# Attention outputs kept as token rows: records in DRAM, merged by token tile, memory keys and values on chip

## What is computed

```python
q = rmsnorm(q.reshape(B, S, N_ATT_HEADS, ATT_HEAD_DIM), q_g)
k = rmsnorm(k.reshape(B, S, N_ATT_HEADS, ATT_HEAD_DIM), k_g)
for g, (window, dilation) in enumerate(DIL_GROUPS):
    o, lse = dilated_window_attention(q[:, :, hs], k[:, :, hs], v[:, :, hs], dilation, radius, slopes[hs])
w = jax.nn.softmax(jnp.stack(lses, axis=0), axis=0)
o = jnp.sum(w[..., None] * jnp.stack(outs, axis=0).astype(jnp.float32), axis=0)
```

## Time and profile before

| | us |
|---|---|
| median of 3 runs (2603.51 to 2604.8) | 2604.01 |
| the profiled execution | 2601.91 |
| its span from first to last instruction | 2600.3 |
| PE busy in the span | 2414.0 |
| DVE busy | 1200.4 |
| ACT busy | 981.0 |
| POOL busy | 444.2 |

### The profile page before, as it was taken

How to read it: one execution, slowest core, us unless ns; L and a number is a source line. 1 busy time by engine, 2 the same in 40 slices (tenths; PEclk the granted TensorE clock), 3 DMA queues, 4 the chain that set the end, 5 groups by cost and what they waited for, 6 DMA issues and landing times. The chain is left out here.

```text
span 2600.3 us, 37949 instructions
## 1 busy us (share of the span) xinstructions
PE 2414.0 (93%) x14495; PEld 2088.1 (80%) x14495; DVE 1200.4 (46%) x1766; ACT 981.0 (38%) x1644; POOL 444.2 (17%) x306
## 2 busy tenths in 40 slices
PE   5999998999899999999989889399999999999997
PEld 4876675666688888888878778289999999999997
DVE  6334346445433230000154443756666666666663
ACT  6333334334510002211120033255565656565553
POOL 0001110110200000000000000123444343434342
PEclk8999998999999999999989999689999999999998
DMA  5310000001011112222155354477888878888872
GB/s 170 101 29 25 17 25 17 17 17 49 1 41 41 35 29 82 91 74 91 67 162 167 127 187 154 155 237 240 253 250 263 252 240 252 250 256 261 253 235 60
DMA packets 328237, 342.67 MB, mean 132 GB/s; under 512 B 11857, under 2 KB 308817, under 8 KB 327633
## 3 DMA queue, kind: packets, MB, share of 16 engines
q1 hardware_dynamic: 315280, 309.96, 37.9%
q0 software_dynamic: 12864, 31.46, 4.6%
HBM read 297.35 MB, written 44.04 MB: 131 GB/s over the span
## 5 line engine op out<-in xcount | busy, mean ns | idle before, releaser
L2042 PE MATMUL bank_pair<-tokens_hi_lo,ehi 128*128 128x320 f32 x2048 | 533.1, 347 | 1.1 <-DVE tokens_hi_lo L1886 1.1
L2043 PE MATMUL bank_pair<-tokens_hi_lo,elo 128*128 128x160 f32 x2048 | 483.5, 236 | 0.0
L2043 PEld LDWEIGHTS bank_pair<-tokens_hi_lo,elo 128*128 128x128 f32 x2048 | 391.9, 191 | 0.0
L2042 PEld LDWEIGHTS bank_pair<-tokens_hi_lo,ehi 128*128 128x128 f32 x2048 | 385.2, 188 | 1.2 <-issue 1.2
L1821 ACT ACTIVATE ehi<-eraw 128x2048 fp32r<-128x2048 f32 x192 | 366.1, 1907 | 12.9 <-DMA eraw<-in_w_eg 10.0
L1879 DVE TENSOR_TENSOR elo<-eraw,ehi 128x2048 fp32r<-128x2048 f32 x144 | 329.1, 2286 | 82.8 <-ACT ehi L1821 82.8
L1797 POOL TENSOR_TENSOR elo<-eraw,ehi 128x2048 fp32r<-128x2048 f32 x47 | 225.0, 4788 | 387.0 <-ACT ehi L1821 387.0
L2042 PE MATMUL bank_pair<-hidden_hi_lo,ehi 128*128 128x320 f32 x1024 | 271.8, 349 | 19.1 <-DVE hidden_hi_lo L1892 19.1
L2043 PE MATMUL bank_pair<-hidden_hi_lo,elo 128*128 128x160 f32 x1024 | 241.4, 236 | 0.0
L2042 PEld LDWEIGHTS bank_pair<-hidden_hi_lo,ehi 128*128 128x128 f32 x1024 | 191.9, 187 | 23.3 <-DVE hidden_hi_lo L1892 22.1
L1206 PE MATMUL bank_pair<-hT_hi,whi 128*128 128x512 f32 (+1 forms) x576 | 204.0, 354 | 1.2 <-PEq L1036 1.2
(11 more groups left out here) (254 smaller groups left out, 4326.7 us busy)
## 6 DMA issues: line engine op xcount, KB each, us to landing
eraw<-in_w_eg SPq DMA_DIRECT2D x64, 1024.0 KB, 7.2
eraw<-in_w_eu SPq DMA_DIRECT2D x64, 1024.0 KB, 5.4
eraw<-in_w_ed SPq DMA_DIRECT2D x64, 1024.0 KB, 5.3
raw<-in_w_in SPq DMA_DIRECT2D x64, 512.0 KB, 4.1
scratch_g<-sig SPq DMA_DIRECT2D x24, 640.0 KB, 3.5
sig<-scratch_g SPq DMA_DIRECT2D x24, 640.0 KB, 3.9
xt<-in_x SPq DMA_DIRECT2D x10, 512.0 KB, 4.5
scratch_m<-acc SPq DMA_DIRECT2D x8, 640.0 KB, 4.9
```

Source lines behind the costliest of these rows:

```text
L2042: nc.tensor.matmul(out, wh, moving[:, k, :], start=(k == 0), stop=False)
L2043: ins = nc.tensor.matmul(out[:, HI], wl, moving[:, k, HI], start=False, stop=(k == KD - 1))
```

## The change

The weights of the combination no longer come from logarithms in rows. V of an attention unit now has the (unnormalised) probabilities as weights and the values as moving operand, so its output has the queries on partitions. ACT copies it into a record `orec` of 132 elements for each query: the 128 outputs of two heads, their negative maxima and their sums. POOL writes each record to DRAM (`save_record`); six records take turns, and `biased_max` of a unit waits until the record six units before is saved. The logarithm, the inverse, the subtraction, the multiplication on POOL and piece L are gone for attention units; they stay, but for L and the subtraction, in memory units.

The groups are merged for each segment of tokens in four stages of a tick each: POOL loads the three groups' records of the segment's tokens (`load_rows`), DVE and ACT take minimum, differences and exponentials (`combine_shifts`), DVE the weights (`combine_weights`), POOL multiplies and adds (`merge_rows`), PE transposes the merged rows (`rows_transposes`) and DVE copies them into `oB` (`rows_copy`). The three segments of a pair share the buffer `orows`. For pair 0 the stages lie in ticks 48 to 57, for pair 1 in ticks 72 to 81. Memory keys and values are written once to `Kx` and `Vx` and stay there. The memory units start at tick 68: 15 of the 20 are under products, five come after them, in ticks 75 and 76. The diff, cut to its core:

```diff
-    OT = at("OT", [P, 3, NT], F32, W)
-    LS = at("LS", [2, 3, NT], F32, W + 15360)
...
+    REC = P + 4
+    OUTS, NMAX, SUMS = slice(0, P), slice(P, P + 2), slice(P + 2, P + 4)
+    NREC = 6
...
+    orows = place("head_rows", [P, 4, 3, REC])
+    Kx = place("Kx", [P, XH, NMEM])
+    Vx = place("Vx", [P, 4, XH * P])
...
+    orec = [place(f"head_record{i}", [P, REC]) for i in range(NREC)]
...
+    scratch_o = nc.dram_tensor("scratch_o", [2, NT, 3, REC], F32, kind="Internal").ap()
...
         if ph % 3 == 2:
-            for i in range(4):
-                ticks[start + room + 1 + i]["combine"].append((ph // 3, i))
-            after = start + room + 5
-    for i in range(n_units - 60):
-        ticks[after + i // 5]["units"].append(60 + i)
+            for n in range(3):
+                for stage in range(4):
+                    ticks[start + room + 4 + 3 * n + stage]["combine"].append((ph // 3, n, stage))
+    for j in range(XH):
+        first_tick = start + 4 + 2 * j + (j == 3)
+        for i in range(5):
+            ticks[first_tick + i // 3]["units"].append(60 + 5 * j + i)
...
-            if u is not None and u < 60:
-                acts.append(("lse", u))
...
-                if c == 11:
-
-                    sp.wait_ge(seg_free, 8)
-                    sp.wait_ge(s_vcp, 4)
-                    sp.dma_start(scratch_kx, Kx_early[:].rearrange("p a b -> p (a b)")).then_inc(s_memout, 16)
-                    sp.dma_start(scratch_vx, Vx_early[:].rearrange("p a b -> p (a b)")).then_inc(s_memout, 16)
-            sp.wait_ge(s_memout, 32)
-            sp.wait_ge(pv_done, N_ATT)
-            sp.dma_start(Kx[:].rearrange("p a b -> p (a b)"), scratch_kx).then_inc(s_memin, 16)
-            sp.dma_start(Vx[:].rearrange("p a b -> p (a b)"), scratch_vx).then_inc(s_memin, 16)
...
-                    nc.scalar.activation(dst, obank[:, 0:P], ACT.Copy).then_inc(o_copied, 1)
+                    nc.scalar.activation(orec[v % NREC][:, OUTS], obank[:, 0:P], ACT.Copy).then_inc(o_copied, 1)
...
+            def save_record(v):
                 un = unit(v)
+                pool.wait_ge(o_copied, v + 1)
+                pool.dma_start(scratch_o[un["pair"], tok(None, un["base"], un["st"]), un["g"], :],
+                               orec[v % NREC][:]).then_inc(rec_saved[v % NREC], 16)
...
+            def load_rows(pr, n):
+                t0, nt = SEGS[n]
+                c = 3 * pr + n
+                if n == 0:
+                    for i in range(NREC):
+                        pool.wait_ge(rec_saved[i], 16 * (30 // NREC) * (pr + 1))
+                if c >= 1:
+                    pool.wait_ge(rows_tr, c)
+                pool.dma_start(orows[:, 0:nt // P],
+                               scratch_o[pr, t0:t0 + nt].rearrange("(n p) g r -> p n g r", p=P)).then_inc(
+                    rows_loaded, 16)
+
+            def merge_rows(pr, n):
+                c, nn = 3 * pr + n, SEGS[n][1] // P
+                rec = orows[:, 0:nn]
+                pool.wait_ge(c_wts, c + 1)
+                for i in range(nn):
+                    heads = rec[:, i, :, OUTS].rearrange("p g (h e) -> p g h e", h=2)
+                    ins = nc.gpsimd.tensor_tensor(heads, heads,
+                                                  c_wt[:, i].unsqueeze(3).to_broadcast([P, 3, 2, E_ATT]), ALU.mult)
+                step(ins)
+                step(nc.gpsimd.tensor_tensor(rec[:, :, 0, OUTS], rec[:, :, 0, OUTS], rec[:, :, 1, OUTS], ALU.add))
+                nc.gpsimd.tensor_tensor(rec[:, :, 0, OUTS], rec[:, :, 0, OUTS], rec[:, :, 2, OUTS],
+                                        ALU.add).then_inc(rows_merged, 1)
+
+            for tk in ticks:
+                for what, v in tk["amid"] + tk["after"]:
+                    if what == "values" and v < N_ATT:
+                        save_record(v)
+                    elif what == "scores" and v >= N_ATT:
+                        normalise(v)
+                for pr, n, stage in tk["combine"]:
+                    if stage == 0:
+                        load_rows(pr, n)
+                    elif stage == 2:
+                        merge_rows(pr, n)
...
-                    dve.wait_ge(p_norm, v - 2)
+                neg = nmax[:, b:b + 2]
                 if un["att"]:
+                    neg = orec[v % NREC][:, NMAX]
+                    if v >= NREC:
+                        dve.wait_ge(rec_saved[v % NREC], 16 * (v // NREC))
...
+            def combine_shifts(pr, n):
+                c, nn = 3 * pr + n, SEGS[n][1] // P
+                rec, lowest = orows[:, 0:nn], c_min[:, 0:nn]
+                dve.wait_ge(rows_loaded, 16 * (c + 1))
+                step(nc.vector.tensor_tensor(lowest, rec[:, :, 0, NMAX], rec[:, :, 1, NMAX], ALU.min))
+                step(nc.vector.tensor_tensor(lowest, lowest, rec[:, :, 2, NMAX], ALU.min))
+                nc.vector.tensor_tensor(c_wt[:, 0:nn], lowest.unsqueeze(2).to_broadcast([P, nn, 3, 2]),
+                                        rec[:, :, :, NMAX], ALU.subtract).then_inc(c_dsub, 1)
...
+            def rows_copy(pr, n):
+                t0, nt = SEGS[n]
+                dve.wait_ge(rows_tr, 3 * pr + n + 1)
+                nc.vector.tensor_copy(oB[:, pr, t0:t0 + nt], tbank[:, 0:nt]).then_inc(rows_cp, 1)
...
-                pe.wait_ge(p_norm, v + 1)
+                if un["att"]:
+                    pe.wait_ge(ex_done, v + 1)
+                else:
+                    pe.wait_ge(p_norm, v - N_ATT + 1)
...
-                            ins = nc.tensor.matmul(obank[64 * h:64 * h + 64, 0:P],
-                                                   V[un["buf"]][0:ln, i, 64 * h:64 * h + 64],
-                                                   PT[v % 2][0:ln, 2 * h + c, :], start=(c == 0),
+                            ins = nc.tensor.matmul(obank[:, 64 * h:64 * h + 64], PT[v % 2][0:ln, 2 * h + c, :],
+                                                   V[un["buf"]][0:ln, i, 64 * h:64 * h + 64], start=(c == 0),
                                                    stop=(c == len(un["keys"]) - 1))
...
+            def rows_transposes(pr, n):
+                pe.wait_ge(rows_merged, 3 * pr + n + 1)
+                free_tbank(("c", 3 * pr + n))
+                for i in range(SEGS[n][1] // P):
+                    ins = nc.tensor.transpose(tbank[:, i * P:(i + 1) * P], orows[:, i, 0, OUTS], ident[:])
+                ins.then_inc(rows_tr, 1)
```

More of the change, by code:

```diff
@@ new lines, in kernel_body, with place @@
+    OUTS, NMAX, SUMS = slice(0, P), slice(P, P + 2), slice(P + 2, P + 4)
+    NREC = 6
+    o = W + 37888
+    def place(name, shape):
+        nonlocal o
+        t = at(name, shape, F32, o)
+        size = 4
+        for n in shape[1:]:
+            size *= n
+        o += -(-size // 32) * 32
+        return t
+    orows = place("head_rows", [P, 4, 3, REC])
+    Kx = place("Kx", [P, XH, NMEM])
+    Vx = place("Vx", [P, 4, XH * P])
+    vT = place("vT", [P, NT])
+    sq = [place(f"sq{i}", [P, 512]) for i in range(2)]
@@ L206, in kernel_body @@
+    Pm = [place(f"Pm{i}", [P, 2, 256]) for i in range(3)]
+    PT = [place(f"PT{i}", [P, 4, P]) for i in range(2)]
+    orec = [place(f"head_record{i}", [P, REC]) for i in range(NREC)]
+    c_min = place("combine_min", [P, 4, 2])
+    c_wt = place("combine_weight", [P, 4, 3, 2])
+    c_part = place("combine_part", [P, 4, 3, 2])
+    c_tot = place("combine_total", [P, 4, 2])
     memT_hi = at("memT_hi", [P, KD, NMEM], F32R, W)
     memT_lo = at("memT_lo", [P, KD, NMEM], F32R, W + 16384)
-    Kx_early = at("Kx_early", [P, XH, NMEM], F32, W + 32768 + 2048 + 1024)
@@ L524, in kernel_body @@
         uses += [("u", v) for what, v in tk["after"] if what == "transposes"]
+        uses += [("c", 3 * pr + n) for pr, n, stage in tk["combine"] if stage == 3]
         for use in uses:
@@ L655, in _, with step @@
         @block.gpsimd
         def _(pool):
-            for v in range(n_units):
+            steps = [0]
+            def step(ins):
+                steps[0] += 1
+                ins.then_inc(c_step, 1)
+                pool.wait_ge(c_step, steps[0])
+            def save_record(v):
                 un = unit(v)
+                pool.wait_ge(o_copied, v + 1)
+                pool.dma_start(scratch_o[un["pair"], tok(None, un["base"], un["st"]), un["g"], :],
+                               orec[v % NREC][:]).then_inc(rec_saved[v % NREC], 16)
@@ L833, in _ @@
                 units_steps(tk["after"])
-                for pr, stage in tk["combine"]:
-                    combine(pr, stage)
+                for pr, n, stage in tk["combine"]:
+                    if stage:
+                        (combine_shifts, combine_weights, rows_copy)[stage - 1](pr, n)
         @block.tensor
@@ L867, in square_sums @@
                                  stop=True).then_inc(ss_done, 1)
-            def bc_before(s):
-                return 9 * sum(1 for tk in ticks[:s + 1] for _, stage in tk["combine"] if stage == 3)
             def v_round(n):
@@ L959, in pv @@
```

(27 more changed lines are left out.)

174 lines of the change are left out of this document (47 added, 127 removed).

## The result

| | before | after |
|---|---|---|
| median of four runs, us | 2604.41 | 2564.16 |
| lowest to highest | 2603.51 to 2605.01 | 2562.72 to 2570.25 |
| span of the profiled execution | 2600.3 | 2563.6 |
| first product of the convolution | 726.00 | 686.75 |

A forecast was written before the change was run, and what follows sets the result against it. PE, busy for 93% of the span, was taken as the bound, so only its own work and waits counted: 17.6 + 23.1 + 2.2 = 42.9 us saved from 2601.91, plus 2.1 for the median, gives 2561; range 2542 to 2583.

The forecast's parts named there:

- Ticks 8 to 44 and 50 to 67: Attention-unit stretches outside pair 0's old combination: 17.6 us saved, from 11.0 + 9.2 - 2.6.
- (1): Ticks 8 to 44 and 50 to 67: the one-row transpose L921 goes, 55 x 0.2 = 11.0 us saved.
- (2): Same ticks: PE's waits for the log-denominator on POOL and its copy on DVE go, 9.2 us saved.
- (b): Rival: the waits of (2) return on the maximum or the exponentials, PE keeps the 9.2; 2570 us, chance 0.12.
- (d): Rival: the six-record ring holds DVE's maximum and PE, 18 us per us of landing beyond 14; chance 0.04.
- (3): Same ticks: V with probabilities as weights, between 7.4 us saved and 13.0 lost; taken as 0.
- rival (c): V doubles in all 60 units, 50.5 us lost: 2611.5 us, slower; chance 0.04.
- (4): Same ticks: fewer DVE and ACT steps, record DMAs: 0; pair 0's transposes and bank waits: 2.6 us lost.
- Rival (a): The end: combination rounds take 22 us each instead of 14, giving 2577 us; chance 0.20.
- 14 + 2 x 14 + 1 to leave the block = 43: The end: first segment's merge done at 14 us, two serial rounds of 14, 1 to leave; 21.2 saved from 64.19.
- The clock term: Start of the convolution: PE begins at its lower clock level, 3.4 us at half speed, 1.7 lost.
- Memory K and V on chip: Memory keys and values no longer go to DRAM and back: worth 0, no PE wait names the reload.

The follow-up runs named there:

- a smaller ring: Changed kernel with five record buffers instead of six: 2566.96 us, ratio 0.9858 to the kernel before.
- the operand experiment: Changed kernel with V's old operand order in the 60 attention units (values as weights, heads side by side): 2568.38 us, ratio 0.9867.
- The experiment with SP: Changed kernel with the sixty record DMAs and six record loads issued by SP instead of POOL: 2560.03 us, ratio 0.9839.
- the packed one: Changed kernel with pair 1's combination packed into ticks 69 to 77, DMAs still on POOL: 2551.05 us, ratio 0.9799.

## Why the prediction was right

**The total is closer than its parts.** The sums were made against the profiled executions, and between these 36.7 were saved (2600.3 to 2563.6) where 42.9 were forecast. That the medians miss by only 3 is partly luck: the profiled execution lay 2.1 below the median before and 1.1 above it after. Of the signs given, the convolution's first product came 39.25 us earlier (42 forecast) and a whole unit's V took 0.81 (0.90).

**Ticks 8 to 44 and 50 to 67, right, with errors that cancel.** (1) The row: 0.2 forecast, 0.145 by putting it back, so 8.1 for 55 of them and not 11.0. (2) The two waits were taken as 9.2, which is their total from 106 to 726; in these ticks the trace of before has 8.0 of them (1.2 and 3.6 for the log-denominator, 2.2 and 1.0 for its copy). They are gone and did not return as others: the wait for the maximum is 1.3 where it was 0.8, and a smaller ring changed nothing, so rivals (b) and (d) fall. No run put these waits back by themselves. (3) V was set at a tie: at equal clock the operand experiment gives 3.2 in favour of the change in these ticks. The parts moved inside the bounds: whole units 0.81 instead of the forecast 0.90; mixed ones 1.35 against 1.44 before:

```profile
273.45 1.42 PE L945 MATMUL bank_pair<-V,PT 128*128 128x64 f32 x8
274.80 0.39 PE L864 MATMUL bank_pair<-hT_hi,whi 128*128 128x256 f32 x1
```

Not counted was what T pays in front of V in the old order. The rule in "TensorEngine Tiling (Array Packing)", When to Use Tiling, of the Trainium skill, which the prediction weighed, holds for V alone in whole units (0.59 against 0.81, not twice), and not for the 60 units together: rival (c) would have needed 50 us. (4) Pair 0's three waits for the bank came to 1.1, 0.8 and 0.7, with 0.5 estimated for each. Added up with these sizes, and with the forecast 1.1 for pair 0's transposes, the parts come to 15.1 of the 16.0 measured.

**Ticks 45 to 49, right:** 35.34 for 36.7, at clock 1.00 where it was 0.86; the broadcasts' own 12 us and their lower clock are gone together, and so are the 8.2 in which PE sat idle there (59.79 less 51.59 busy).

**Ticks 68 to 73, right:** 68.7 for 69. A part of it is chance: tick 68 took 12.39 in this execution and 10.78 with the smaller ring. PE is idle for 2.04 on a memory unit's exponentials in both; what differs is the clock behind that wait:

```profile
569.89:582.28 12.39, 10.35 (x60) 8.96 (x60) 5.74 (x10) 7.35 (x26) 3.66 (x5) 0.87 0.19 59
```

```profile
569.84:580.62 10.78, 8.74 (x60) 7.66 (x60) 5.18 (x9) 6.77 (x23) 3.36 (x5) 1.00 0.20 61
```

**The end: the mechanism right, a term of the sum mis-sized.** Twice idle, each time released by POOL's merge, but 5.28 and 11.35 where 10 or more was forecast for both: the prediction gave PE 1 to 4 us of work in a round, and in the first it was on memory units until 661.23, 8.5 into it. The rounds came out near the 14: the loads took 4.9 and 4.8 (5.3 forecast), POOL's merges 5.9 (5.4). Rival (a), 22 a round, falls. The sum "14 + 2 x 14 + 1 to leave the block = 43" failed in its 1: leaving the block took 4.95, because the change also moves DMAs onto POOL in a block that had none there. The experiment with SP brings it to 1.4. The trace of before could have told: the drain in the earlier trace rows's block, whose DMAs POOL issues, took 3.78, and 1.14 where POOL issues none. By its parts the stretch is 14.1 + 15.2 + 13.9 + 4.95: the other 1.2 is in the first round. Its steps on DVE and ACT took 2.9 (657.62 to 660.51) and those of the second 1.9, as forecast (1.8): DVE also had a memory unit's probabilities to copy in between. Its transposes and the hand-off to the next load took 1.4 (666.51 to 667.93) at the lower clock. The clock term was 1.7 and came to 2.4.

**Memory K and V on chip** was costed at 0. No run took this part out alone, so that stays argued and is not shown: no wait of PE for it is named before or after.

The changed kernel left much of what its end could give unclaimed: the experiments that moved pair 1's combination show 13, and 23 with SP's DMAs.

## What to carry to other kernels

When work is moved under a product, look at what then ends the stage: here 17.0 were lost where the moved units went and 16.0 won at the end, until the serial chain behind them was started earlier. A step that is put early enough is not yet hidden: see what stands behind it on each in-order engine, since a 5.9 us merge delays the divisions queued behind it. That cost PE a wait of 3.0 with the merge in tick 75 and none with it in tick 73. When DMAs are moved to POOL, look at the drain at the end of that block, and at blocks of the same trace in which POOL already issues some.

## What the runs showed that was not expected

POOL's drain at the end of the block lasts to about 5.5 us past its last arithmetic if POOL issued DMAs in the block: 6.78 in all, in after and in five of the experiments, and 8.46 in the packed one, where two divisions follow the last add. It ends with the last add if SP issued them (1.36). The last of POOL's DMAs had been issued 11 us before (667.93) and its rows were in use on DVE from 672.77, so it is not this transfer that the drain waits for.

The order of V's operands changes the price of the transposes before it, 0.59 or 0.49 for four, though they are the same instructions.
